# Output projection of a decoder layer as seven block products per pair of token tiles, in one block of programs with gate and up

## What is computed

```python
def reference(x, norm_mix, w_in, q_norm, k_norm, conv_w, w_out, norm_ffn, w_gate, w_up, w_down):
...
        mix = jnp.concatenate([attn, conv], axis=-1)
        x = x + mix @ w_out[l].astype(mix.dtype)
        h = _rms_norm(x, norm_ffn[l])
        g = h @ w_gate[l].astype(h.dtype)
        u = h @ w_up[l].astype(h.dtype)
        x = x + (jax.nn.silu(g) * u) @ w_down[l].astype(h.dtype)
    return x
```

## Time and profile before

| | us |
|---|---|
| median of 3 executions | 2661.15 (2657.15 to 2662.24) |
| the profiled execution | 2662.36 |
| its span in the profile | 2660.5 |
| PE busy | 2518.8 |
| DVE, ACT, POOL busy | 1303.8, 1139.8, 1239.7 |
| mean granted clock of TensorE | 0.981 |

### The profile page before, as it was taken

The page is one execution under the profiler, slowest core; times in us unless marked ns, Lnnn a source line. Parts: engine busy times, 40 slices in busy tenths (PEclk is TensorE's granted clock), DMA queues, the critical chain, the costliest instruction groups (busy, mean ns, idle before and its releaser), DMA issues.

```text
span 2660.5 us, 34870 instructions
## 1 busy us (share of the span) xinstructions
PE 2518.8 (95%) x12272; PEld 2082.3 (78%) x12272; DVE 1303.8 (49%) x1315; ACT 1139.8 (43%) x1857; POOL 1239.7 (47%) x865
## 2 busy tenths in 40 slices
PE   8999879999899999799799999999999999999999
PEld 6788657777777777678678888888887888888887
DVE  4433346776676677534564544432534545442222
ACT  3222256766676677432343333322433333332322
POOL 1212156767667676301375544423486455442332
PEclk9999989999999999899899999999999999999999
DMA  5665573343533522254422122256543222214554
GB/s 174 192 186 158 159 195 98 109 131 99 145 90 94 157 73 66 89 166 143 158 80 94 60 83 95 94 165 207 190 145 101 95 71 79 87 63 154 166 190 154
DMA packets 299865, 336.03 MB, mean 126 GB/s; under 512 B 17888, under 2 KB 239072, under 8 KB 298720
## 3 DMA queue, kind: packets, MB, share of 16 engines
q1 hardware_dynamic: 299744, 334.57, 41.0%
HBM read 240.13 MB, written 94.37 MB: 126 GB/s over the span
## 4 chain that ended last, share of the span: by engine, by line
PE 48%; POOL 1%; DMA 1%; DVE 0%; ACT 0%; issue 0%; SPq 0%; ACTq 0%; DVEq 0%
PE ffn_ps L1791 10%; PE ffn_ps L1793 10%; PE ffn_ps L1795 10%; PE ffn_ps L76 6%; PE ffn_ps L77 6%; PE ffn_ps L78 6%; POOL ffn_A L1731 1%; DMA ffn_raw<-in_w_up 1%; ACT ffn_A L1461 0%; DVE ffn_raw L1601 0%; DVE ffn_raw L1611 0%; DVE ffn_raw L1606 0%; DVE ffn_s L1647 0%; DVE ffn_s L1597 0%; ACT ffn_s L1473 0%
## 5 line engine op out<-in xcount | busy, mean ns | idle before, releaser
L1731 POOL TENSOR_TENSOR ffn_A<-ffn_raw,ffn_A 128x512 fp32r<-128x512 f32 x264 | 364.7, 1392 | 379.0 <-ACT ffn_A L1461 378.7
L1791 PE MATMUL ffn_ps<-all_B,ffn_A 128*128 128x512 f32 x1232 | 481.3, 391 | 17.9 <-POOL ffn_A L1731 15.8
L1793 PE MATMUL ffn_ps<-all_B,ffn_A 128*128 128x512 f32 x1232 | 480.7, 390 | 0.0
L1795 PE MATMUL ffn_ps<-all_B,ffn_A 128*128 128x512 f32 x1232 | 480.6, 390 | 0.0
L829 DVE TENSOR_TENSOR_SCAN att_stick<-att_z,att_stick 128x128 f32<-128x128 f32 (+5 forms) x192 | 331.2, 1726 | 221.8 <-ACT att_z L741 210.5
L875 POOL TENSOR_TENSOR att_a<-att_a,att_stick 128x128 f32<-128x128 f32 (+5 forms) x192 | 281.6, 1472 | 215.3 <-DVE att_stick L829 214.5
L1736 POOL TENSOR_TENSOR ffn_A<-ffn_A_over,ffn_A 128x512 fp32r<-128x512 f32 x88 | 160.3, 1821 | 333.7 <-ACT ffn_A L1494 333.7
L1791 PEld LDWEIGHTS ffn_ps<-all_B,ffn_A 128*128 128x128 f32 x1232 | 232.3, 189 | 67.4 <-POOL ffn_A L1731 19.1
L1639 DVE TENSOR_TENSOR ffn_A<-ffn_A_over,ffn_A 128x1024 fp32r<-128x1024 f32 x88 | 117.3, 1333 | 322.2 <-ACT ffn_A L1492 322.2
L76 PE MATMUL ffn_ps<-ffn_A 128*128 128x512 f32 x704 | 273.9, 389 | 0.0
L77 PE MATMUL ffn_ps<-ffn_A 128*128 128x512 f32 x704 | 273.9, 389 | 0.0
(11 more groups left out here) (122 smaller groups left out, 5035.7 us busy)
## 6 DMA issues: line engine op xcount, KB each, us to landing
ffn_A_over<-in_w_down SPq DMA_DIRECT2D x88, 512.0 KB, 3.5
att_w_stage<-in_w_in SPq DMA_DIRECT2D x48, 512.0 KB, 4.4
ffn_raw<-in_w_gate SPq DMA_DIRECT2D x22, 1024.0 KB, 6.7
ffn_raw<-in_w_up SPq DMA_DIRECT2D x22, 1024.0 KB, 8.8
hidT<-ffn_s SPq DMA_DIRECT2D x88, 256.0 KB, 2.4
ffn_A_over<-hidT SPq DMA_DIRECT2D x88, 256.0 KB, 3.7
qkv_x_t<-in_x SPq DMA_DIRECT2D x16, 512.0 KB, 4.5
hT_hi<-qkv_hT_hi SPq DMA_DIRECT2D x16, 512.0 KB, 5.4
```

Source lines behind the costliest of these rows:

```text
L1731: nc.gpsimd.tensor_tensor(A[:, j, p, 1, :, :], operand(j, p), A[:, j, p, 0, :, :].bitcast(F32), ALU.subtract).then_inc(lo_done, 1)
L1791: nc.tensor.matmul(ps[:, b, :], A[:, j, p, 0, k, :], B[p][:, 0, k, :], start=first_mm, stop=False, skip_group_check=True)
L1793: nc.tensor.matmul(ps[:, b, :], A[:, j, p, 0, k, :], B[p][:, 1, k, :], start=False, stop=False, skip_group_check=True)
L1795: mm = nc.tensor.matmul(ps[:, b, :], A[:, j, p, 1, k, :], B[p][:, 0, k, :], start=False, stop=last_mm, skip_group_check=True)
```

## The change

`back_stage` takes the place of both stages, so that output projection, gate and up and down are one block of programs in which no engine waits for all the others.

*The output projection in seven products.* The 16 token tiles become eight pairs. Per pair the 256 x 1024 block of mixT is the A operand (stationary), w_out in four quarters the B operand, and seven block products of 12 matmuls give the pair's two tiles: 56 products, 672 matmuls. Each product goes to a bank of its own turn (MIX_BANK) and is added by DVE to the x tile in SBUF (`add`, L1650), seven additions per pair of 128 x 512. The first two pairs are interleaved in the order OPENING, the later ones take PAIR_ORDER.

*Three fills of B.* w_out is fill 0, h of tokens 0 to 1023 fill 1, of tokens 1024 to 2047 fill 2. HOME says for each fill which region holds which operand, so that a fill's loads can start as each region's last product of the fill before ends (`wait_free`). Each fill takes two or four loads, four differences on DVE (t_part, L1692), one copy (L1434) and seven roundings (b_hi, L1442) on ACT, and seven lo parts (b_lo, L1222), three on POOL and four on DVE, in fill 0 two on POOL and five on DVE. Fill 1 is made between output projection and gate and up, fill 2 between rounds 10 and 11 of gate and up, beside their products.

*The normalised tiles.* ACT squares a tile into PSUM, POOL makes the root, ACT scales the tile by it in place (`normalize`), PE transposes it, and DVE evacuates it with the gain applied. All 16 tiles go to h2T in DRAM and come back from there. An x tile is loaded into the place that the h tile of two pairs before has left (load_x).

*The order of the phases.* Gate and up run their 22 rounds without a break, then down runs its four groups as the last phase.

The core of the diff, tables first:

```diff
-B_AT = [24, 26, 28, 30, 32, 34, 36]
+FREED = [P1, P5, P6, P7, P2, P4, P3]
+PAIR_ORDER = [P1, P5, P6, P2, P7, P3, P4]
+OPENING = [(0, P1), (1, P1), (0, P2), (1, P2), (0, P5), (1, P5), (0, P6), (1, P6),
+           (0, P7), (0, P3), (0, P4), (1, P7), (1, P3), (1, P4)]
+MIX = OPENING + [(m, p) for m in range(2, TILE_PAIRS) for p in PAIR_ORDER]
+SLOT = {P1: 0, P5: 3, P6: 1, P2: 0, P7: 3, P3: 1, P4: 2}
+MIX_BANK = {P1: 0, P6: 0, P7: 0, P4: 0, P2: 1, P5: 2, P3: 2}
+def refilled(freed):
+    return dict(zip((P1, P3, P7, P5, P6, P2, P4), freed))
+LO_ON_POOL = [(P2, P3), (P2, P4, P3), (P2, P4, P3)]
+LO_ON_DVE = [(P1, P5, P6, P7, P4), (P1, P5, P6, P7), (P1, P5, P6, P7)]
+        def wait_free(eng, f, region):
+            if f == 0:
+                return
+            p = {i: p for p, i in HOME[f - 1].items()}[region]
+            if f == 1:
+                eng.wait_ge(m_prod_done, MIX_AT[TILE_PAIRS - 1, p] + 1)
+            else:
+                eng.wait_ge(prod_done, NP * (ROUNDS - 1) + 1 + max(spot[GATE, p], spot[UP, p]))
...
+            def load_x(mm, i):
+                c = 2 * (mm % 2) + i
+                wait(sp, h_stored[c], DMA * (mm // 2))
...
+            def pair_product(n):
+                mm, p = MIX[n]
+                j = mm % 2
+                pe.wait_ge(m_lo_done, n + 1)
+                if mm == 0:
+                    wait_b_lo(pe, 0, p)
+                if p == P1:
+                    wait(pe, added, MIX_AT[mm - 2, P4] + 1 if mm >= 2 else 0)
+                elif p in (P2, P5):
+                    wait(pe, added, MIX_AT[mm - 2, {P2: P2, P5: P3}[p]] + 1 if mm >= 2 else 0)
+                    wait(pe, ss_done, 2 * (mm - 1))
+                else:
+                    pe.wait_ge(added, MIX_AT[mm, {P6: P1, P7: P6, P4: P7, P3: P5}[p]] + 1)
+                block_product(3 * j + MIX_BANK[p], j, p, HOME[0][p], p in (P1, P2, P5)).then_inc(m_prod_done, 1)
...
             def keep(R, j, n):
                 act.wait_ge(prod_done, NP * R + 1 + spot[j, (P1, P6, P7)[n]])
...
+            pair_hi(0)
+            pair_hi(1)
+            b_hi(0, P1)
+            pair_hi(2)
+            pair_hi(3)
+            b_hi(0, P2)
+            copy(0)
+            b_hi(0, P5)
+            pair_hi(4)
```

More of the change, by code:

```diff
@@ L1536, in _ @@
-            opening()
-            for G in range(HALVES):
-                for c in range(ROUNDS):
-                    R = ROUNDS * G + c
-                    if R == 0:
-                        continue
-                    last = c == ROUNDS - 1
-                    more = R + 1 < HALVES * ROUNDS
-                    ahead = more and not last
+            pair_hi(0)
[5 more added lines that the diff above has]
+            copy(0)
@@ new lines, in _ @@
+            last_pair = TILE_PAIRS - 1
+            b_hi(1, P6)
+            square(last_pair, 1)
+            copy(1)
+            hi(0, 11)
+            keep(0, GATE, 0)
+            normalize(last_pair, 0)
+            normalize(last_pair, 1)
+            b_hi(1, P7)
+            b_hi(1, P2)
+            hi(0, 12)
+            keep(0, UP, 0)
+            keep(0, GATE, 1)
+            hi(0, 13)
+            b_hi(1, P4)
+            keep(0, UP, 1)
+            b_hi(1, P3)
+            for R in range(LAST + 1):
+                ahead = R < LAST
+                if R:
@@ new lines, in _ @@
+                if R == 0:
+                    hi(1, 3)
+                    hi(1, 4)
+                elif ahead:
+                    hi(R + 1, 7)
+                silu(R, 1)
+                if R == ROUNDS - 1:
+                    b_hi(2, P1)
+                if R == 0:
+                    hi(1, 5)
+                    hi(1, 6)
+                elif ahead:
+                    hi(R + 1, 8)
+                silu(R, 2)
+                if ahead:
+                    for n in range(9 if R else 7, 12):
+                        hi(R + 1, n)
@@ new lines, in _ @@
+            dve.wait_ge(gain_in, DMA)
+            for i in range(7, NM):
+                if i + 7 < NM:
+                    if i % 7 < 4:
+                        pair_sum(i // 7 + 1, (P5, P7, P6, P3)[i % 7])
+                else:
+                    k = i - (NM - 7)
+                    if k in (0, 1, 3, 4):
+                        sums(0, k // 3, P5 if k % 3 == 0 else P7)
+                    if k == 5:
+                        sums(0, GATE, P6)
+                        t_part(1, 0)
+                    if k == 6:
+                        sums(0, UP, P6)
+                        lo_b(1, P1)
+                add(i)
+                for mm in range(TILE_PAIRS):
+                    for t in range(2):
+                        if i == TILE_DONE[mm][0] + 3 + t:
+                            evacuate(mm, t)
@@ new lines, in transposes @@
+            def transposes(mm, i):
+                t = 2 * mm + i
+                pe.wait_ge(xn_done, t + 1)
+                for n in range(2):
+                    wait(pe, h_done, 2 * (t - 1) + n + 1)
+                    for k in range(4):
+                        c = n * BANK + k * P
+                        last = nc.tensor.transpose(ps[:, 6 + n, k * P:(k + 1) * P], s_tile(mm % 2, i)[:, c:c + P],
+                                                   cst["ident"][:, :])
+                    last.then_inc(tr_full, 1)
```

1047 lines of the change are left out of this document (554 added, 493 removed).

## The result

The changed kernel takes 2680.26 us (median of 4, 2678.44 to 2682.16) against 2660.53 before in the same comparison: ratio 1.0076, 95% interval 1.0058 to 1.0093. It is slower by 19.7 us; 24 were forecast, and 2685 lay within 5 us. The profiled execution took 2681.3, its span is 2679.4.

A forecast was written before the change was run, and what follows sets the result against it. TensorE was taken as the bound, busy 2518.8 of 2660.5 us. Terms -21.8 + 3.3 + 24.3 + 0.7 + 14.4 + 10.5 = +31.4, less 7.1, gave +24: about 2685 us, range 2660 to 2704.

The forecast's parts named there:

- What goes: Output projection: 768 matmuls become 672, 96 at 0.2267 us each, -21.8 us, all on the path.
- Exclusion of DVE and POOL: In the new fills, DVE instructions with two SBUF inputs and POOL instructions lock each other out for whole instructions.
- Rival 1: DVE and POOL overlap after all; shorter gaps in opening, between stages and at the turn: 2652 us, chance 0.12.
- The start: Before the first product: 1.5 MB in 7.5 us, ACT 1.9, DVE 2.3, 11.8 against 8.5 us: +3.3.
- The opening: First two pairs of the output projection: gaps of 7.7 before (0,P5), 10.1 before (0,P6) and small ones: +24.3 us.
- the walk: Engine queues stepped through in code order; 11% too long for the kernel before, so 7.1 us taken off new gaps.
- Into gate and up: From output projection to gate and up: gaps of 9.0, 5.4, 4.2, 1.7, 0.4; 20.7 against 20.0 us: +0.7.
- The turn: Gate and up, round 10 to 11, third fill beside products: gaps 1.8, 3.2, 1.2, 9.6 us; +14.4.
- The clock: PE drops from 2.4 to 1.2 GHz behind gaps: nine drops instead of four, 2.1 us each, +10.5 us.
- Rival 3: The opening never reaches the upper clock, as gaps come every two products: +26, 2711 us, chance 0.07.
- Rival 4: Pair stage not gap-free: x tiles load late, 2.5 us in each of five later pairs, +12, 2698 us, chance 0.07.
- Rival 2: Chains shorter than walked, half the new gaps and drops: about 0 to +10, 2667 us, chance 0.14.

The follow-up runs named there:

- e2: Changed kernel with POOL's three lo parts of the third fill each issued as four instructions of 512 columns: 2679.38 us.
- e4: Changed kernel with the lo part of P2 of fill 0 made by DVE ahead of its sums, not by POOL: 2677.58 us.
- e8: Changed kernel with the first quarter of w_out asked for before the first mixT blocks: 2677.78 us.
- e7: Changed kernel with P4's difference and P6's lo part ahead of P7's difference on DVE in the opening: 2680.17 us.
- e6: Changed kernel with B's P1 of fill 1 moved ahead in ACT's and DVE's queues, before gate and up: 2682.95 us.
- e1: Changed kernel without the third fill of B; the second half of gate and up uses the first half's operands: 2662.11 us.
- e11: Changed kernel with the old order of phases, third fill under down and all seven of its lo parts on POOL: 2664.31 us.
- e3: Changed kernel with ACT copying out the bank of (gate,P7) before two roundings of round 12, in round 11 alone: 2676.96 us.
- e9: Changed kernel with 90, 58, 72, 72 and 68 identity transposes on PE in five waits: 2676.62 us.
- e5: Changed kernel with shorter series of identity transposes on PE in the same five waits, 64 before the first product: 2679.33 us.

## Why the prediction was right

- **What goes** was right: the stage has 672 matmuls, and where nothing waits they run at 0.227 us.
- **Exclusion of DVE and POOL** was right (the after-profile's 5 us sums, e2, e4). Rival 1 falls. In the opening it decides (e4). At the turn the chain "3 x 4.6 + 1.3, with DVE between 17.6 us" took 16.6 (1779.56 to 1796.17, where DVE's waiting sum starts): the three lo parts 14.9, the rest POOL's first split of round 12. Of that POOL's own work is 13.8 + 1.3, and freeing DVE gave nothing (e2). So exclusion adds some 1.5 us to this wait. The prediction put 8.6 of the turn's 16.5 down to it (rival 1's walk has 7.9); how much it costs in the smaller gaps ahead wasn't tried.
- **The start**, +3.3, measured +5.2. The step that failed is "1.5 MB: 7.5 us". ACT could start on the quarter of w_out 9.3 us behind the first load (1105.51 to 1114.79); asked for first, 7.5 us at most (e8, 1106.73 to 1114.26). By 1109 us the changed kernel has asked for 1.5 MB beyond what the first product needs. SP stood 6.4 us in issuing the third pair of mixT loads, but that is behind the loads which the first product needs, and whether the later loads slow the earlier ones wasn't tried:

```profile
1105.51 0.95 SPq L1256 DMA_DIRECT2D ffn_raw<-mixT  x2
1106.51 0.50 SPq L1237 DMA_DIRECT2D all_B_over<-in_w_out  x1
...
1109.01 6.38 SPq L1256 DMA_DIRECT2D ffn_raw<-mixT  x2
```

- **The opening**: gaps 7.7 and 10.1 forecast, 6.8 and 8.4 measured; of the small ones (2.5, 0.5, 1.1, 2.0, 3.1) three of 2.0, 2.2 and 1.2 came. All in all 27.1 forecast, 20.6 measured: the walk was 31% too long there, not 11%. The chains to the two large ones were walked better than that: from the first product to (0,P5) 20.9 us forecast and 20.5 measured, from there to (0,P6) 17.8 and 16.7. More than half of the difference lies in the small ones behind. That the two large gaps are work and not order is shown by e7 alone, for the second.
- **Into gate and up**: 9.0 forecast, 8.5 + 0.7 measured, right, with its cause (e6). The gaps of 5.4 before (up,P6) and 4.2 in the second round came out at 1.9 and 2.3, the 1.7 of the last pair's tiles at 0.4, and one of 1.7 before (up,P4) wasn't forecast: 20.7 us forecast and 15.5 measured. Why these chains were shorter wasn't tried.
- **The turn**: 1.8, 3.2, 1.2, 9.6 forecast, 0.9, 2.9, 1.3, 8.0 measured; e1 and e11 confirm the place and the price, e3 the chain through the bank. The 0.7 at the start of down didn't come.
- **The clock**: nine falls at 2.1 forecast, ten at 1.8 measured, +10.5 and +10.6. That the two agree is in part luck. The prediction took from one wait of 2.14 us without a fall that such waits are free, and three of the ten falls came behind waits of 1.85, 2.00 and 2.19 us; and the excess of the other profiles would have given 1 to 4 us less. As a price by itself this term was misleading: the walk's gaps already stood behind slow matmuls, and with two of the three falls up to (0,P6) taken away, (0,P5) and (0,P6) start as late as with them (e9). Rival 3 (the opening stays at the lower level) fell, as it came back 3 to 6 us behind each wait.
- **Rival 4** fell: 94 of 94 us busy. Rival 2 was right in part: 29.5 us of added gaps came, where the three gap terms and the start add up to 42.7 (35.6 with the 7.1 taken off) and rival 2's to 17.3. Between output projection and gate and up its -5 was the better number (-4.5 measured). Without the 7.1 the forecast would have been 31, so the 11% learnt from the kernel before did most for the final number, though it was not the same share in every stage.

## What to carry to other kernels

Replacing eight block products by seven saves matmul time only where the operands for it can be made beside other products; here two small stages (two pairs of tiles, one change of fill) each made PE wait for nearly what the whole stage saves. A refill of operands belongs under a phase whose other engines have time to spare: the same fill cost some 16 to 18 us between two rounds (e11, e1), and under down there is no wait, only one of 2.1 us behind it (e11). And before an order is changed to close a gap, add up the work of the engines behind it: two reorderings here closed 5 us each and got them back within 30 us, while moving 4.6 us of POOL's work to 2.3 of DVE's was a gain.

## What the runs showed of the hardware

- A DVE instruction of 0.69 us with both operands in SBUF takes 5.0 us beside one on POOL that takes 4.6 alone and 1.7 beside one of 1.26 (e2): the other engine's longest instruction is the price.
- TensorE's level also fell behind short waits, and late: behind one of 1.85 us (1345.39) the matmuls were fast for 1.3 us and then took 0.43 from 1346.68 to 1349.24; behind 2.14 us in the kernel before they weren't slow at all, and in e11, in the same place, they were (0.75 for the first). Which it is can't be told from the length of the wait alone.
- Behind nearly the same waits, the number of slow matmuls changes from one execution to the next: 6 to 12 behind the first product.
- Work on PE that computes nothing holds the upper level: 68 transposes of the identity in an 8 us wait, and the next matmuls took 0.23 (e9). In e5, whose transposes left 2.8 to 4.5 us idle, it didn't. It gains time only where no later wait of PE, for a chain of the other engines, takes it back.
- The stages that no kernel here changes ended up to 6 us apart between profiles (1097.7 to 1103.9 us), more than most edits are worth.
